# Nine modulation vectors of a two-block model computed on GpSimd instead of TensorE, and shorter splits of small weight tiles

## The reference, cut to what matters

```python
for i in range(DEPTH):                                   # DEPTH = 2
    m_lat = (jax.nn.silu(c) @ ada_w[i] + ada_b[i])[:, None, :]        # ada_w[i]: 1024 x 9*1024
    m_ctx = (jax.nn.silu(c_ctx) @ ada_w[i] + ada_b[i])[None, None, :]
    sh1, sc1, gt1, sh2, sc2, gt2, sh3, sc3, gt3 = jnp.split(m_lat, N_MOD, axis=-1)
    ...
    x = x + 0.5 * gt1 * swiglu(modulate(x, g1, sh1, sc1), ffn1_wi[i], ffn1_wo[i])
    ...   # layer 0: convolution, layer 1: attention; then the second FFN
```

## Time and profile before

| | us |
|---|---|
| median of 3 runs | 3325.91 (3325.67 to 3328.05) |
| the profiled execution | 3331.19 |
| its span, first to last instruction | 3329.4 |
| TensorE busy in it | 3183.1 |
| DVE busy | 1967.4 |
| ACT busy | 1352.4 |
| GpSimd busy | 2.3 |
| granted TensorE clock, mean | 0.979 of full |

### The profile page before, as it was taken

One profiled execution on the slowest core, in us unless ns is written; L12 is line 12 of the kernel. 1 busy time (PEld: TensorE's weight loads), 2 busy tenths in 40 slices (PEclk: granted clock), 3 DMA queues, 4 the chain that ended last, 5 costly groups with the idle time before them and its releaser, 6 DMA issues.

```text
span 3329.4 us, 50055 instructions
## 1 busy us (share of the span) xinstructions
PE 3183.1 (96%) x21085; PEld 2793.4 (84%) x21085; DVE 1967.4 (59%) x3119; ACT 1352.4 (41%) x2052; POOL 2.3 (0%) x6
## 2 busy tenths in 40 slices
PE   8999899998999899997999999899999999999999
PEld 8989789998999889996888866578887888874898
DVE  6677667666667666666433479853335433455555
ACT  4444345455444445445322242432224222337544
POOL 0000000000000000000000000000000000000000
PEclk9999899999999999998999999999999999999999
DMA  7765536746785535855333243243334333242563
GB/s 203 225 207 163 160 122 193 215 137 179 225 231 173 178 102 168 236 160 167 101 102 93 84 127 101 89 139 90 101 92 124 114 94 96 89 139 76 165 184 108
DMA packets 672217, 478.88 MB, mean 144 GB/s; under 512 B 22527, under 2 KB 671097, under 8 KB 671993
## 3 DMA queue, kind: packets, MB, share of 16 engines
q1 hardware_dynamic: 671993, 475.68, 47.9%
HBM read 474.57 MB, written 1.05 MB: 143 GB/s over the span
## 4 chain that ended last, share of the span: by engine, by line
PE 78%; DVE 11%; ACT 5%; DVEq 3%; issue 1%; DMA 1%; SPq 0%; ACTq 0%
PE ps L613 23%; PE ps L615 23%; PE ps L614 23%; DVE wl L1580 3%; DVE Pp L1573 3%; ACT wh L1139 2%; DVEq L2107 1%; PE ps L691 1%; PE ps L1090 1%; DVE Hl L1573 1%; PE ps L1067 1%; DVE Xx L1573 1%; PE ps L674 1%; DMA raw<-in_w_in 1%; DVEq L1643 1%
## 5 line engine op out<-in xcount | busy, mean ns | idle before, releaser
L1580 DVE TENSOR_TENSOR wl<-raw,wh 128x1024 fp32r<-128x1024 f32 x780 | 951.1, 1223 | 867.1 <-ACT wh L1139 866.2
L1139 ACT ACTIVATE wh<-raw 128x1024 fp32r<-128x1024 f32 x780 | 815.7, 1056 | 1451.1 <-PE ps L615 1326.9
L613 PE MATMUL ps<-Fh,wh 128*128 128x256 f32 (+1 forms) x3200 | 976.5, 305 | 14.9 <-DVE Fl L2129 5.6
L614 PE MATMUL ps<-Fl,wh 128*128 128x256 f32 (+1 forms) x3200 | 971.0, 303 | 0.0
L615 PE MATMUL ps<-Fh,wl 128*128 128x256 f32 (+1 forms) x3200 | 970.9, 303 | 0.0
L613 PE MATMUL ps<-Hh,wh 128*128 128x256 f32 (+1 forms) x2672 | 909.3, 340 | 47.8 <-DVE Hl L1573 13.8
L615 PE MATMUL ps<-Hh,wl 128*128 128x256 f32 (+1 forms) x2672 | 892.7, 334 | 0.0
L614 PE MATMUL ps<-Hl,wh 128*128 128x256 f32 (+1 forms) x2672 | 892.7, 334 | 0.0
L613 PEld LDWEIGHTS ps<-Fh,wh 128*128 128x128 f32 x3200 | 614.3, 192 | 49.1 <-issue 16.1
L614 PEld LDWEIGHTS ps<-Fl,wh 128*128 128x128 f32 x3200 | 614.4, 192 | 23.1
L615 PEld LDWEIGHTS ps<-Fh,wl 128*128 128x128 f32 x3200 | 614.1, 192 | 23.4
(11 more groups left out here) (290 smaller groups left out, 2125.9 us busy)
## 6 DMA issues: line engine op xcount, KB each, us to landing
raw<-in_ffn_w_in SPq DMA_DIRECT2D x176, 512.0 KB, 5.4
raw<-in_ffn_wi SPq DMA_DIRECT2D x176, 512.0 KB, 5.2
raw<-in_ada_w SPq DMA_DIRECT2D x144, 512.0 KB, 4.6
raw<-in_w_in SPq DMA_DIRECT2D x112, 512.0 KB, 4.9
raw<-in_ffn_w_out SPq DMA_DIRECT2D x64, 512.0 KB, 4.7
raw<-in_ffn_wo SPq DMA_DIRECT2D x64, 512.0 KB, 4.3
raw<-in_ffn_w_out SPq DMA_DIRECT2D x32, 384.0 KB, 3.8
raw<-in_ffn_wo SPq DMA_DIRECT2D x32, 384.0 KB, 3.7
```

The lines of the kernel that those rows point to most:

```text
L613: nc.tensor.matmul(o, wh[:, u.par, kc, w], xh(kc), start=(kc == 0), stop=False)
L614: nc.tensor.matmul(o, wh[:, u.par, kc, w], xl(kc), start=False, stop=False)
L1139: nc.scalar.activation(tile_of(wh[:, u.par], t), tile_of(raw[:, u.slot], t), ACT.Copy) \
L1580: V.tensor_tensor(tile_of(wl[:, u.par], t), tile_of(raw[:, u.slot], t), tile_of(wh[:, u.par], t).bitcast(F32), ALU.subtract).then_inc(lo_d ...
```

## The change

Nine of the 18 batches stay on TensorE: one in each of the two norms before block 1's mixers, and seven in block 2 (its start, five norms and before the second pointwise product). The other nine are computed on GpSimd during block 2's first three FFNs, which are those on 512 columns. GpSimd multiplies each of a member's 8 row groups by the two conditioning values of each partition (`tensor_scalar`, 256 elements per partition) and adds it up (`tensor_tensor`), with a drain between dependent steps. That is 16 products, 14 sums and 14 drains for a member, 36 members in all. The member's slot is free when its last sum is done, and SP waits for `mod_added`. After four members TensorE sums over the partitions (`sum_modulation`, 8 fp32 matmuls of a picking column block by the sums, 128x32 by 128x256). Copy, turn and keep follow as before. Each member stands two units after the last one. The order of the vectors is changed a little (`VECTORS`), and `keep_modulation` now computes the factors of its vector at once. The late splits around the removed batches are no longer late. `hi` and `lo` process only as many row groups as a unit has (`depth`).

```diff
+ADDED_FFNS = (K_SECOND, K2_FFN2, K2_L1)
 def batch_places():
+    out = [(K_MIX,) * BATCH, (K_LAYER + K_MIX,) * BATCH, (K_SECOND,) * BATCH]
+    for k, ends in zip(ADDED_FFNS, ((K2_CONV, K2_PW2, K2_FFN2), (K2_L1,), (K2_KV, K2_FFN4))):
+        for j in (4, 12, 20):
+            out.append(tuple(k + j + 2 * m for m in range(BATCH)))
+        out += [(end,) * BATCH for end in ends]
+    return out
...
+SUM_AT = {places[-1] + 1: b for b, places in SPREAD.items()}
+COPY_AT = {places[-1] + 2: b for b, places in SPREAD.items()}
+TURN_AT = {places[-1] + 3: b for b, places in SPREAD.items()}
+KEEP_AT = {places[-1] + 4: b for b, places in SPREAD.items()}
...
-        return self.k - 1 in BATCH_AT or self.k == K2_WO + 1
+        return self.k - 1 in BATCH_AT
+    def depth(self):
+        if self.k < K_SECOND and self.k % K_LAYER >= K_PLE:
+            return C if (self.k % K_LAYER - K_PLE) % 2 == 0 else PLE // P
+        for first in FFN_STARTS:
+            if first + FFN_UNITS - 4 <= self.k < first + FFN_UNITS:
+                return GROUPS[2]
+        return C
...
                 if i is None:
                     sp.wait_ge(lo_done, Unit(k).lo_done(1))
+                elif i in ADDED:
+                    sp.wait_ge(mod_added, ADDED[i] + 1)
                 else:
                     sp.wait_ge(mod_mm, i + 1)
...
+            pool.wait_ge(c_there, 1)
+            for n, b in enumerate(SPREAD):
+                if n >= 2:
+                    pool.wait_ge(mod_mm, BATCH * (list(SPREAD)[n - 2] + 1))
+                for m in range(BATCH):
+                    u, acc = ModUnit(b, m), sums_at(b)
+                    pool.wait_ge(raw_full[u.slot], u.raw_full())
+                    for kc in range(C):
+                        for s in range(2):
+                            c = cs[:, kc, 2 * (BATCH - 1) + s:2 * (BATCH - 1) + s + 1]
+                            o = acc[:, m, s, :] if kc == 0 else product[:, s, :]
+                            nc.gpsimd.tensor_scalar(o, raw[:, u.slot, kc, :], c, None, ALU.mult)
+                        pool.drain()
+                        if kc == 0:
+                            continue
+                        for s in range(2):
+                            ins = nc.gpsimd.tensor_tensor(acc[:, m, s, :], acc[:, m, s, :], product[:, s, :], ALU.add)
+                        if kc < C - 1:
+                            pool.drain()
+                    ins.then_inc(mod_added, 1)
...
+            def sum_modulation(b):
+                pe.wait_ge(mod_added, ModUnit(b, BATCH - 1).added())
+                pe.wait_ge(mod_kept, b)
+                for s in range(2):
+                    for m in range(BATCH):
+                        r = 2 * m + s
+                        mm = nc.tensor.matmul(ps[32 * m:32 * m + 32, 5, 0:256], co[:, CO_PICK + 7 - r:CO_PICK + 39 - r],
+                                              sums_at(b)[:, m, s, :], start=(s == 0), stop=(s == 1))
+                mm.then_inc(mod_mm, BATCH)
...
-                gates_batch = BATCH_AT[k + 20]
-                pe.wait_ge(rg_tanh, l * 8 + 8)
-                modulation(gates_batch, range(BATCH))
...
-                if j == 3:
-                    modulation(BATCH_AT[K2_CONV + 4], range(BATCH))
...
-                if i == 0:
-                    modulation(BATCH_AT[K2_KV + 5], range(BATCH))
...
-                nc.scalar.activation(tile_of(wh[:, u.par], t), tile_of(raw[:, u.slot], t), ACT.Copy) \
+                n = u.depth()
+                nc.scalar.activation(tile_of(wh[:, u.par], t, n), tile_of(raw[:, u.slot], t, n), ACT.Copy) \
...
-                V.tensor_tensor(tile_of(wl[:, u.par], t), tile_of(raw[:, u.slot], t),
-                                tile_of(wh[:, u.par], t).bitcast(F32), ALU.subtract).then_inc(lo_done, 1)
+                n = u.depth()
+                V.tensor_tensor(tile_of(wl[:, u.par], t, n), tile_of(raw[:, u.slot], t, n),
+                                tile_of(wh[:, u.par], t, n).bitcast(F32), ALU.subtract).then_inc(lo_done, 1)
...
-                if i == 8:
-                    for u in (Unit(K2_WO), Unit(K2_WO + 1)):
-                        hi(u, 0, True)
-                        hi(u, 1, True)
```

More of the change, by code:

```diff
@@ L66 @@
 K_GATES, K_V = K_MIX + 20, K_MIX + 16
+FFN_STARTS = tuple(l * K_LAYER + j for l in range(DEPTH) for j in (0, K_FFN2)) + (K_SECOND, K2_FFN2, K2_L1, K2_FFN4)
 MOD_UNITS = N_MOD * D // 256
 BATCH = 4
+ADDED_FFNS = (K_SECOND, K2_FFN2, K2_L1)
 def batch_places():
[L75 to L83, removed]
+    out = [(K_MIX,) * BATCH, (K_LAYER + K_MIX,) * BATCH, (K_SECOND,) * BATCH]
[4 more added lines that the diff above has]
+    return out
+VECTORS = (0, 1, 2, 3, 4, 5, 6, 7, 8, 9, 10, 12, 11, 13, 15, 16, 14, 17)
 BATCHES = batch_places()
@@ L164, in __init__, with added @@
         self.slot = self.raw % 4
-        self.l, self.index = divmod(BATCH * b + m, MOD_UNITS)
+        self.l, self.index = divmod(BATCH * VECTORS[b] + m, MOD_UNITS)
     def raw_full(self):
         return 32 * (self.raw // 4 + 1)
-    def done(self):
-        return BATCH * self.b + self.m + 1
+    def added(self):
+        return ADDED[BATCH * self.b + self.m] + 1
 def deferred(norm):
@@ L310, in build @@
         kraw = Gb[:].rearrange("p c t -> p (c t)")[:, 0:1024].rearrange("p (n t) -> p n t", n=2)
+        sums_of = [b.rearrange("p c t -> p (c t)").rearrange("p (m s n) -> p m s n", m=BATCH, s=2) for b in (QK[:, 0], QK[:, 1])]
+        product = Vb[:, 1, 512:1024].rearrange("p (s n) -> p s n", s=2)
         kdup = Kb[:].rearrange("p c t -> p (c t)").rearrange("p (n t) -> p n t", n=KVH)
@@ L492, in load_members @@
                     wait_for_slot(u)
-                    for h in (1, 0):
+                    for h in (0, 1) if i in ADDED else (1, 0):
                         a = h * (C // 2)
@@ L1648, in norm, with scale_const, gate_const @@
                     lo(Unit(after + 1), 1, True)
+            def scale_const(l, i):
+                r = R_NORM + (3 * l + i) * C
+                for s in range(2):
+                    stt(S1[:, i, :, s], MOD[:, l, (3 * i + 1) * C:(3 * i + 2) * C, s], 1.0, par[:, 2, r:r + C],
+                        ALU.add, ALU.mult)
+            def gate_const(l, i):
+                factor = 0.25 if i != 1 else (0.5 if l == 0 else 1.0)
+                V.tensor_scalar(G1[:, i], MOD[:, l, (3 * i + 2) * C:(3 * i + 3) * C, :], factor, None, ALU.mult)
             def keep_modulation(b):
@@ L2032, in _ @@
                     lo(u.later(2), 1)
-            def scale_const(l, i):
-                r = R_NORM + (3 * l + i) * C
-                for s in range(2):
-                    stt(S1[:, i, :, s], MOD[:, l, (3 * i + 1) * C:(3 * i + 2) * C, s], 1.0, par[:, 2, r:r + C],
-                        ALU.add, ALU.mult)
-            def gate_const(l, i):
-                factor = 0.25 if i != 1 else (0.5 if l == 0 else 1.0)
-                V.tensor_scalar(G1[:, i], MOD[:, l, (3 * i + 2) * C:(3 * i + 3) * C, :], factor, None, ALU.mult)
             def gain(i):
@@ L2053, in shift @@
                 return lambda kc, s: MOD[:, l, (3 * i) * C + kc, s:s + 1]
-            for i in range(3):
-                scale_const(0, i)
-                gate_const(0, i)
-            dve.drain()
             rms(8, T)
```

89 lines of the change are left out of this document (24 added, 65 removed).

## The result

The changed kernel takes 3531.9 us (median of 4 runs, 3530.6 to 3535.3) where the kernel before takes 3326.3 us in the same session: a ratio of 1.062, interval 1.060 to 1.064. The forecast was 3278 us with a range up to 3377. The profiled execution has a span of 3529.0 us, 199.6 us more than before, and its mean granted clock is 0.954 (0.979 before).

A forecast was written before the change was run, and what follows sets the result against it. TensorE, busy 96% of the span, was taken to bound the FFNs by matmul count, others elsewhere. Terms -21.8 - 20 - 6.6 - 1 - 9 + 9.8 + 1 = -47.6 us took 3325.91 to 3278 us; range 3263 to 3377.

The forecast's parts named there:

- At 17 us nobody waits, so Pool costs 0: Block 2's three FFNs: a Pool member takes 17 us, under the 24.1 us limit, so no waiting time is added.
- Rival 1: Pool is late in block 2's FFNs, holding up weight loads and TensorE: 3377 us; chance 0.30 of late enough to matter.
- DVE's exclusion: Pool stands still during DVE's two-operand instructions in block 2's FFNs: 6.1 us per member, making 23.1 us.
- Members on TensorE: Each spread member costs 1.09 us; twenty removed from block 1's FFNs give -21.8 us.
- Attention: Block 2's attention: batch copy ahead of ACT's normalisation and four late splits leave the chain, -6.6 us (-3.8 to -8).
- Gates: Block 1's gates: removing the batches saves 9.4 and 10.7 us, together -20 us; -10 if DVE cannot start earlier.
- Rival 2: Gains given back: DVE bounds the heads and ACT the patch stage, 20 us lost, 3298 us; chance 0.10.
- Rival 3: TensorE's sums break the stream more than members do: 9 x 2 us more, 3296 us; within a shared chance of 0.10.
- Patch stages: Short splits shorten one low part per chain turn: 8 pairs x 0.8 us, 6 us gained.
- FFN ends: Two short units near the chain, each 0.27 us shorter on DVE and ACT: 3 us for eight FFNs (0 to 6).
- Convolution: Convolution: the removed batch's TensorE work is mostly hidden under DVE's taps, -1 us (0 to -3.9).
- SP's loads waiting over 100 us in all: Sign that the forecast is wrong: SP's weight loads wait for Pool over 100 us in all.

The follow-up runs named there:

- e_six: Changed kernel, but GpSimd multiplies and sums only 6 of 8 row groups of each member; 3288.9 us, 0.988 of the kernel before.
- e_wide: Changed kernel with both conditioning values in one 512-element GpSimd instruction, products as tensor_tensor with broadcast operands; 3289.1 us, 0.989 of the kernel before.
- e_tt: Changed kernel with its 256-element products as tensor_tensor with the constant broadcast, instruction count unchanged; 3361.0 us, 1.010 of the kernel before.
- e_seven: Changed kernel, but GpSimd multiplies and sums only 7 of 8 row groups of each member; 3406.5 us, 1.024 of the kernel before.
- e_mem: Changed kernel, but in block 2 DVE fills the low parts with zeros instead of subtracting; 3414.2 us, 1.026 of the kernel before.
- e_copy: Changed kernel, but in block 2 DVE copies the weight tile as low part instead of subtracting; 3458.6 us, 1.040 of the kernel before.
- e_pe: Changed kernel, but the twelve members of each of the three FFNs run on TensorE, without sums; 3324.2 us, 0.9986 of the kernel before.
- e_short: Kernel before with only the short splits added; 3315.9 us, 0.997 of the kernel before.
- e_half: Changed kernel, but GpSimd computes only one of the two conditioning vectors; 3289.4 us, 0.988 of the kernel before.
- e_port: Kernel before plus ten members' GpSimd work in each of block 2's first three FFNs, which nobody waits for; 3326.3 us, ratio 1.0003.

## Why the prediction was wrong

**The failing step is the size of Pool's member, in the prediction's words "At 17 us nobody waits, so Pool costs 0".** The mechanism stood in the prediction as Rival 1: no cost to a limit of 24.1 us, then 33 us of time per us of T, the wait in SP's queue for freed slots and in TensorE for the sum. The runs bear out both numbers: T, the time of a member, is the one that decides. With 3289 us for the change without waiting:

| Kernel | own work, us | T, us | time over 3289, us | for each us of T over 24.1 |
|---|---|---|---|---|
| e_six | 19.8 | 23.6 | 0 | |
| e_wide | 19.4 | 23.3 | 0 | |
| e_tt | 21.7 | 26.2 | 72 | 34 |
| e_seven | 23.4 | 27.4 | 117 | 36 |
| e_mem | 27.0 | 27.6 | 125 | 36 |
| e_copy | 27.0 | 29.1 | 170 | 34 |
| changed kernel | 27.0 | 30.9 | 243 | 36 |

The slope is 34 to 36 where 33 was taken: three FFNs with twelve members rather than eleven between the first load and the last sum. The limit comes out of the same runs: the changed kernel's first FFN is 87.2 us longer, 5.3 of them the price without waiting, and (87.2 - 5.3) / 12 = 6.8 us a member, so the wait begins at 24.1. But T was put at 17 us and was 30.9. By terms: 16 products at 0.91 us from start to start instead of 0.42, 14.6 us instead of 6.7; 14 sums at 0.73 instead of 0.63, 10.2 instead of 8.8; 15 gaps for drains of 0.15, 2.2 instead of 1.5 (for 14 drains, a price that no row gave); and 3.9 us instead of none for DVE. More than half of the error of 13.9 us (7.9) is the product. Even its upper bound, three passes at the memset's rate, was too low: 0.74 us, and for the whole member 24.3 us where the own work is 27.0. A rate read from a memset doesn't bound a product with a constant from SBUF on Pool, and the bound should have been called a guess.

**DVE's exclusion is the smaller part.** Without nearly all of it (e_mem, T = 27.6) the kernel is still 88 us slower than before; the own work alone is over the limit. But with the product as e_tt has it (0.61 us, between two and three passes by the scale of the earlier trace rows) T is 26.2 us, 4.5 of them DVE's, and the kernel slower than before too. So the chance of 0.30 for Rival 1 was low even for one who priced the product nearly right. The exclusion was put at 6.1 us per member if it is complete. In the changed kernel it was 3.9, some two thirds: DVE's instruction and Pool's overlap in part. The Trainium skill's page SBUF — State Buffer (section Who interferes with whom) names the rule that a DVE instruction with two SBUF inputs and Pool exclude each other; the trace agrees in kind, not in full size, and e_copy shows a copy with one input in the way too, which the section has for a copy in a mode that uses both of DVE's port pairs; no run shows whether this one was in such a mode. The forecast took the rule in and found 23.1 us, inside the limit by 1.0; with the right own work either case is over it. The skill's page GPSIMD Engine Reference (section 3.1, Elementwise) gave an estimate of 0.56 us for a sum's 256 elements before the fixed part; the trace agrees, since from 256 elements (0.73 us) to 512 (1.29) a sum grows by 0.56, which leaves 0.17 fixed. The section has no figure for a tensor_scalar.

**The other terms.** The gain was there, but for 11 us: 3289 where the wait stays away, against 3278. About 4 us of it are the difference between profile and median (5.3 us for before, 1.5 for e_wide), which no stage shows and which the prediction took to be the same for both. Members on TensorE: 1.09 us was the distance of the neighbours alone; the next matmul is late too (0.34 instead of 0.23 in e_pe's row), so 1.20 us, and with each batch goes a turn, which the prediction had moved "at about the same price" and so had counted neither in block 1 nor in block 2. In block 1 this made -29.1 of -24.8, in block 2 +15.9 of +10.8: nine sums and nine turns. That the two errors nearly cancel is luck. Attention: -6.6 was expected; -4.2 came in the changed kernel, -2.3 in e_pe and -0.4 in e_wide and e_six. But e_short, whose attention is that of the kernel before, has -2.1 there, so no run shows what the change gives in this stage. Why it differs among kernels that are alike there stays open; this is the other part of the 11 us. Gates: -18.5 against -20, so the loss of half to DVE didn't come. Rival 2 was to give back 20 us at gates and patch stages, which isn't seen; what is missing lies elsewhere. Rival 3 falls: a sum costs what a member costs, its neighbours in e_wide standing 1.32 us apart too; three sums at 1.20 and three turns at 0.46 are 5.0 of the 5.3 us of a stage. Patch stages: -9.6 against -6; e_short gives -4.8 for each with nothing else changed, in a stage of 4.5 turns of which each is 0.8 shorter, so the rest (some 1.2 us a stage) comes at its ends, which was not looked into. FFN ends: -3 was taken; block 1's are -3.3 in e_short, of which 1.2 may be no effect, as said there. The ends of the prediction's terms add up to 3269 to 3297, not to the 3263 to 3295 that it gives. Convolution -0.4 against -1.

**What would show it.** Most signs served: the clock dropping in these FFNs (0.90) and Pool instructions of 0.7 us or more (0.73 and 0.92). The sign of SP's loads waiting over 100 us in all (849) does not separate right from wrong: e_wide has 362 us and e_six 472, and neither loses any by it. DVE's low parts showed not as gaps before Pool's instructions but as longer ones. Of the runs with the places of the change, "Pool's spacing is set by the loads" came only in e_half; e_six and e_wide stay below the limit with Pool never idle.

## What to carry to other kernels

Before moving work to an engine that hardly runs in the profile, find the point from which someone waits for it, and ask whether any row of the trace has that instruction in that form; if none has, give its price a bound that covers a factor of two, or measure it alone first, since below the limit the move is free and above it each us is paid once per use (here 36 times). On Pool prefer one wide tensor_tensor with a broadcast constant to two narrow tensor_scalars: 1.04 us for 512 products against 1.82. With a ring of buffers filled by one in-order queue, count entries: a slow consumer is prefetched only if its next item comes within the ring's depth.

## What the runs showed of the hardware that was not expected

- On Pool a product of 128x256 fp32 with a constant from SBUF takes 0.92 us as a tensor_scalar and 0.61 us as a tensor_tensor with the constant broadcast; 128x512 takes 1.04 us. Sums of two SBUF operands take 0.73 us (256) and 1.29 us (512).
- Pool and DVE hold each other up in both directions: Pool loses 3.9 us in 30.9 beside DVE's subtractions, 2.1 in 29.1 when the low parts are copies that read one operand, and 0.6 in 27.6 when they are memsets, none of it beside the memsets themselves; DVE's subtraction of 128x1024 goes from 1.22 us on average to 1.29 (e_port), 1.33 (changed kernel) and 1.57 beside the wide instructions of e_wide, and one of 128x512 from 0.68 to 0.91 in the first two and 1.42 in the third.
- That contention is free as long as both have slack: ten members' worth of Pool work in each of three FFNs moved no stage by more than 0.04 us (e_port).
